# Block one of a two-block model: `w_out` and `w_ffn_out` multiplied with tokens on partitions, post-norm by token rows, result turned back

## The reference, cut to what matters

```python
h = _rmsnorm(x, g_pre_mix[l]); z = h @ w_in[l]      # then Fourier mix, window attention, memory attention
y = jnp.concatenate([norms of the three groups], axis=-1) @ w_out[l]      # [512, 1024] @ [1024, 1024]
x = x + _rmsnorm(y, g_post_mix[l])
h = _rmsnorm(x, g_pre_ffn[l])
gate, up = jnp.split(h @ w_ffn_in[l], 2, axis=-1)
f = (jax.nn.silu(gate) * up) @ w_ffn_out[l]                               # [512, 2816] @ [2816, 1024]
x = x + _rmsnorm(f, g_post_ffn[l])
```

## Time and profile before

| | us |
|---|---|
| time, median of 3 (lowest to highest) | 3827.07 (3824.5 to 3827.53) |
| profiled execution: its own time | 3827.03 |
| its span | 3825.2 |
| TensorE busy | 3566.6 (93%) |
| VectorE busy | 2516.5 (66%) |
| ScalarE busy | 1642.6 (43%) |
| mean granted TensorE clock, share of full | 0.966 |

### The profile page before, as it was taken

How to read it: one execution, slowest core, us unless ns; L and a number is a source line. 1 busy time by engine, 2 the same in 40 slices (tenths; PEclk the granted TensorE clock), 3 DMA queues, 4 the chain that set the end, 5 groups by cost and what they waited for, 6 DMA issues and landing times.

```text
span 3825.2 us, 50169 instructions
## 1 busy us (share of the span) xinstructions
PE 3566.6 (93%) x19603; PEld 2959.6 (77%) x19603; DVE 2516.5 (66%) x3593; ACT 1642.6 (43%) x2391; POOL 49.4 (1%) x67
## 2 busy tenths in 40 slices
PE   6888999888999899999899999999999989999998
PEld 4566997556898689887467789889988646788986
DVE  6548872745885498647766588639864776658853
ACT  3434552343554355424432445425542443235542
POOL 0000000000000000000000000000000000000000
PEclk8988999898999899999899999999999999999999
DMA  4112332121233223332113223232323211232331
GB/s 127 67 33 67 100 105 95 62 66 44 89 101 101 74 89 111 104 92 72 44 44 87 89 89 109 97 101 91 111 94 99 75 33 56 77 99 89 104 101 60
DMA packets 341622, 320.42 MB, mean 84 GB/s; under 512 B 10969, under 2 KB 334757, under 8 KB 341413
## 3 DMA queue, kind: packets, MB, share of 16 engines
q1 hardware_dynamic: 337204, 307.94, 25.5%
q0 software_dynamic: 2560, 8.26, 0.6%
q10 hardware_dynamic: 1648, 1.34, 0.1%
HBM read 315.40 MB, written 2.10 MB: 83 GB/s over the span
## 4 chain that ended last, share of the span: by engine, by line
PE 71%; DVE 14%; issue 11%; ACT 3%; DMA 0%; POOL 0%; ACTq 0%; DVEq 0%; POOLq 0%
PE products L712 40%; PE products L801 19%; PE small L801 3%; PE products L976 2%; DVE conv L2433 2%; DVE w_lo L1774 1%; ACT w_hi L1256 1%; DVE seven_x L1943 1%; PE small L841 1%; PE products L998 1%; PE products L860 1%; DVE X L1789 1%; DVE x_sums L1932 1%; DVE prob L2353 1%; PE products L1065 1%
## 5 line engine op out<-in xcount | busy, mean ns | idle before, releaser
L1774 DVE TENSOR_TENSOR w_lo<-raw,w_hi 128x2048 fp32r<-128x2048 f32 x192 | 439.9, 2292 | 564.1 <-ACT w_hi L1256 562.9
L1256 ACT ACTIVATE w_hi<-raw 128x2048 fp32r<-128x2048 f32 x192 | 367.3, 1914 | 974.6 <-PE products L712 974.6
L712 PE MATMUL products<-a_hi,w_hi 128*128 128x512 f32 (+1 forms) x1424 | 586.7, 412 | 58.4 <-DVE a_lo L1829 31.9
L712 PE MATMUL products<-a_lo,w_hi 128*128 128x512 f32 (+1 forms) x1424 | 574.2, 403 | 0.0
L712 PE MATMUL products<-a_hi,w_lo 128*128 128x512 f32 (+1 forms) x1424 | 573.5, 403 | 0.0
L801 PE MATMUL products<-seven_x,w_hi 128*128 128x256 f32 x2592 | 469.2, 281 | 8.4 <-DVE w_lo L1972 3.8
L712 PE MATMUL products<-h_lo,w_hi 128*128 128x512 f32 x1056 | 418.6, 396 | 0.0
L712 PE MATMUL products<-h_hi,w_lo 128*128 128x512 f32 x1056 | 418.6, 396 | 0.0
L712 PE MATMUL products<-h_hi,w_hi 128*128 128x512 f32 x1056 | 418.6, 396 | 0.0
L801 PEld LDWEIGHTS products<-seven_x,w_hi 128*128 128x128 f32 x2592 | 397.5, 189 | 12.2 <-DVE w_lo L1972 5.1
L712 PEld LDWEIGHTS products<-a_hi,w_hi 128*128 128x128 f32 (+1 forms) x1424 | 273.3, 192 | 145.0 <-issue 61.0
(11 more groups left out here) (384 smaller groups left out, 6273.9 us busy)
## 6 DMA issues: line engine op xcount, KB each, us to landing
raw<-in_ffn_w SPq DMA_DIRECT2D x240, 512.0 KB, 4.3
raw<-in_w_in SPq DMA_DIRECT2D x108, 512.0 KB, 4.9
raw<-in_w_ffn_in SPq DMA_DIRECT2D x88, 512.0 KB, 4.4
raw<-in_w_out SPq DMA_DIRECT2D x32, 512.0 KB, 4.2
raw<-in_w_ffn_out SPq DMA_DIRECT2D x32, 512.0 KB, 4.1
raw<-in_ffn_w SPq DMA_DIRECT2D x32, 384.0 KB, 3.5
raw<-in_w_ffn_out SPq DMA_DIRECT2D x16, 384.0 KB, 3.5
raw<-in_w_mem_kv SPq DMA_DIRECT2D x8, 512.0 KB, 4.1
```

What stands on the lines that cost most here:

```text
L712: mm = pe.matmul(G[pair][0:m, into + b, 0:n], w[:, s, at:at + m], x, start=(first or into > 0) and k == 0 and q == 0, stop=(last or ends) ...
L1256: act.activation(w_hi[:, s, :], raw[:, s, :], ACT.Copy).then_inc(hi_ready, 1)
L1774: dve.tensor_tensor(w_lo[:, s, :], raw[:, s, :], w_hi[:, s, :].bitcast(F32), ALU.subtract).then_inc(lo_ready, 1)
```

## The change

The two matrices are multiplied the other way round: the operand is the stationary side (128 tokens by 128 input channels), the weights are the moving side (512 output channels wide), and the result has tokens on partitions. It is made in two halves of 512 output channels, four banks each (four tiles of 128 tokens): half 0 in the four `G` banks, half 1 in `B4` to `B7`. The number of products is the same. Units are now 4 input chunks by 512 columns; `w_ffn_out` has one short unit (2 chunks, 24 products) at the end of half 0 and one at the start of half 1. The last unit of half 1 goes token tile by token tile.

ScalarE squares each bank with a running sum over its row (so no adds). The roots are then one number per partition and token tile: VectorE combines both halves, GpSimd takes the power on a 128x1 column, VectorE scales both banks of the tile from PSUM to `y_tok` in SBUF. TensorE turns 32 tiles of 128x128 back into the eight banks. Then VectorE has one operation a chunk, `xT = bank * gain + xT`, in place of two. The split of F1 is moved: on ScalarE from ahead of the post-norm to behind the eight high parts (`late_unit`), on VectorE to behind the eight low parts. The loops of these stages are written out. Removed: `copy_and_square`, `sum_channels` and `spread` of the post-norms, `y_ffn`.

```diff
+MIX_UNITS = (((2, 3, 4, 5), (0, 1, 6, 7)), ((2, 3, 4, 5), (0, 1, 6, 7)))
+FF_FOURS = tuple(tuple(range(k, k + 4)) for k in range(0, FC - 2, 4))
+FF_UNITS = (FF_FOURS + ((FC - 2, FC - 1),), ((FC - 2, FC - 1),) + FF_FOURS)
...
+        def token_banks(p):
+            return ([G[p][:, 0, :], G[p][:, 1, :], G[1 - p][:, 0, :], G[1 - p][:, 1, :]], [B4[:], B5[:], B6[:], B7[:]])
...
+            def by_tokens(hi, lo, halves, before):                      # TensorE
...
+                for half, (banks, units) in enumerate(zip(token_banks(p), halves)):
+                    for u, chunks in enumerate(units):
+                        take_unit()
+                        s, last = (c.unit - 1) % 2, u == len(units) - 1
+                        order = [(n, t) for n in range(len(chunks)) for t in range(TC)]
+                        if half and last:
+                            order.sort(key=lambda at: at[1])
...
+                            for q, (x, w) in enumerate(((hi, w_hi), (lo, w_hi), (hi, w_lo))):
+                                mm = pe.matmul(banks[t], x[:, k, t * P:(t + 1) * P], w[:, s, n * SEQ:(n + 1) * SEQ],
...
+                            if last and n == len(chunks) - 1:
+                                mm.then_inc(tok_done, 1)
...
+                pe.wait_ge(y_scaled, scaled + 2)
+                for i in range(4):
+                    for t in range(2):
+                        turn(i, t)
+                pe.wait_ge(y_scaled, scaled + 3)
+                for i in range(6):
+                    for t in (2,) if i < 4 else range(3):
+                        turn(i, t)
+                pe.wait_ge(y_scaled, scaled + 4)
+                for i in range(DC):
+                    for t in (3,) if i < 6 else range(4):
+                        mm = turn(i, t)
+                    mm.then_inc(z_ready, 1)
...
-                if post_norm:
-                    c.one("sq_used", DC)
-                    sum_channels()
-                    spread()
...
+            def operand(gain, l, squares=True, late_unit=True):         # ScalarE
...
+                if late_unit:
+                    split_hi()
                 if squares:
                     squares_of_x()
...
+            def by_tokens(halves):                                      # ScalarE
...
+                    for t in range(TC):
+                        act.wait_ge(tok_done, c.next("tok_done"))
+                        act.activation(X[:, t, :], banks[t], ACT.Square,
+                                       accum_out=stats[:, 0, half * TC + t:half * TC + t + 1]).then_inc(
...
+            def by_tokens(halves, gain, l, next_gain):                  # VectorE
...
+                for t in range(TC):
+                    dve.wait_ge(stat_ready, c.next("stat_ready"))
+                    root = mean_sq[:, t:t + 1]
+                    dve.scalar_tensor_tensor(root, stats[:, 0, TC + t:TC + t + 1], 1.0 / D, stats[:, 2, t:t + 1],
+                                             ALU.mult, ALU.add).then_inc(pow_asked, 1)
+                    dve.wait_ge(pow_done, c.next("pow_done"))
+                    dve.tensor_scalar(y_tok[:, t, 0:SEQ], first[t], root, None, ALU.mult)
+                    dve.tensor_scalar(y_tok[:, t, SEQ:D], second[t], root, None, ALU.mult).then_inc(y_scaled, 1)
+                banks = turned_banks(p)
                 for i in range(DC + 1):
                     if i < DC:
...
+                        dve.wait_ge(z_ready, c.next("z_ready"))
+                        dve.scalar_tensor_tensor(xT[:, i, :], banks[i], col(gain, l, i), xT[:, i, :],
+                                                 ALU.mult, ALU.add).then_inc(x_ready, c.one("x_ready"))
...
+                        lows_of_x(i - 1, *next_gain)
+                dve.wait_ge(tok_done, c.next("tok_done", TC))
+                split_lo()
...
+            def token_roots():                                          # GpSimd
...
+                    pool.tensor_tensor(root, root, minus_half[:, i:i + 1], ALU.pow).then_inc(pow_done, 1)
```

More of the change, by code:

```diff
@@ L1088, in _, with before @@
                 sum_groups(totals[2:])
[L1090 to L1103, removed]
+                def before(u, n, t, k):
+                    if t:
+                        return
+                    if (u, n) == (1, 2):
+                        spread_groups(totals[2:], (B6[:],))
+                    pe.wait_ge(al_ready, c.next("al_ready"))
+                by_tokens(a_hi, a_lo, MIX_UNITS, before)
                 ffn(True)
@@ L1440, in ffn @@
                             group_skipped()
[L1442 to L1449, removed]
+            def by_tokens(halves):
+                for half, (banks, units) in enumerate(zip(token_banks(c.group % 2), halves)):
+                    for _ in units[1:]:
+                        unit_done()
+                    if not half:
+                        act.wait_ge(tok_done, c.now("tok_done") + TC)
+                        split_hi()
+                    for t in range(TC):
+                        act.wait_ge(tok_done, c.next("tok_done"))
+                        act.activation(X[:, t, :], banks[t], ACT.Square,
+                                       accum_out=stats[:, 0, half * TC + t:half * TC + t + 1]).then_inc(
+                                           stat_ready, c.one("stat_ready"))
+                    act.wait_ge(stat_ready, c.now("stat_ready"))
             def latent_attention(leave):
@@ L1903, in normalised @@
                 low(n - 1)
[L1905 to L1907 removed]
+            def by_tokens(halves, gain, l, next_gain):
+                p = c.group % 2
+                first, second = token_banks(p)
+                for half, units in enumerate(halves):
+                    for u in range(len(units) - 1):
+                        piece()
+                        split_lo()
+                        if half and u == 0:
+                            dve.wait_ge(stat_ready, c.next("stat_ready", TC))
+                            stepped(dve.tensor_scalar(stats[:, 2, 0:TC], stats[:, 0, 0:TC], 1.0 / D, EPS, ALU.mult, ALU.add))
+                    if not half:
+                        dve.wait_ge(tok_done, c.next("tok_done", TC))
+                        split_lo()
+                settled()
+                for t in range(TC):
[6 more added lines that the diff above has]
+                    dve.tensor_scalar(y_tok[:, t, SEQ:D], second[t], root, None, ALU.mult).then_inc(y_scaled, 1)
+                banks = turned_banks(p)
```

116 lines of the change are left out of this document (64 added, 52 removed).

## The result

The changed kernel takes 3788.32 us (median of 4 runs, 3785.62 to 3793.4), the kernel before in the same session 3825.78 (4 runs, 3822.81 to 3827.53). The ratio is 0.9904 [0.9887, 0.9922]: 37.5 us less. The forecast was 3780.6, a gain of 46.4, and faster by over 0.2% with 0.95; the time lies in the range, 7.7 us from the forecast. The profiled execution took 3790.08 with a span of 3788.3, where before it was 3827.03 and 3825.2. TensorE is busy for 3569.0 us, as good as before (3566.6); what went is its idle time.

What follows compares the result with a forecast made beforehand. TensorE, busy 93%, was taken to idle behind each post-norm matrix's last product, 18.9 us at four places. Gains 3 x 12.2 + 9.8 = 46.4 off 3827.03 gave 3780.6 us, range 3773 to 3798.

Steps and rivals of the forecast that it cites:

- E: End of the last product of a post-norm matrix; the forecast's times are in us behind it.
- F0's clock: First 8 of F0's 48 products at the low clock as before, so F0 is through at about 19 us.
- wait at the sum: TensorE's idle time at the pre-norm's sum in F1, until VectorE's adds are done: 0.8 us.
- sum in F1: Pre-norm's sum inside F1, set by VectorE's adds: 24.3 us against 36.5, 12.2 gained at three post-norms.
- layer 0: memory tile: Behind layer 0's FFN, F1's second `memory_tile` waits for ScalarE's copy; TensorE goes on at 25.1 us, idle nearly 3.
- layer 0: gain: Behind layer 0's FFN: 11.3 us gained, less 1.5 for low clock after TensorE's idle time, 9.8.
- A: Rival: operand chunks don't overlap, 2.2 us each and not 1.33; gain 6 a place, 3805 us; chance 0.14.
- B: Rival: `w_ffn_out`'s short units or a late weight stall, up to 2 x 4 us, 3789; chance 0.05.
- C: Rival: with weights moving, each of 1440 products takes longer, e.g. 0.28 us for 0.235, 3846 us; chance 0.03.
- D: Rival: no gain, something later such as weights holds F2 or the next stage; chance 0.02.
- the clock also falls while F1 waits at the sum, 1.5 in each of three places: Smaller rival: low clock behind TensorE's wait at the pre-norm's sum, 1.5 us in three places, 3785 us.
- the likeliest case: The forecast's sum as it stands, chance 0.76; bounds on power, scaling, transposes, clock and hand-overs give 3776 to 3790.

Runs made afterwards that it cites:

- e1: The changed kernel unaltered, run and profiled once more: 3791.01 us, ratio 0.9902 to the kernel before.
- e9: The kernel before the change, unaltered, profiled once more: 3826.92 us, ratio 1.0005.
- e7: The changed kernel with eight unread products put ahead of the pre-norm's sum in F1, in the three places with a plain F1: 3778.28 us, ratio 0.987.
- e2: The changed kernel with the pre-norm's sum in F1 behind product 24 instead of 18, in the three plain places: 3774.45 us, ratio 0.9863.
- e5: The changed kernel with sum later, ScalarE's F1 split earlier, and behind layer 0's FFN later memory tiles and sum: 3769.04 us, ratio 0.9848.
- e8: Half of the change against the kernel before: `w_out` changed, the FFNs of block one as before: 3807.52 us, ratio 0.9944.
- e4: The changed kernel with the pre-norm's sum behind 24 products and ScalarE's split of F1 ahead of the high parts: 3775.57 us, ratio 0.9861.
- e10: The same kernel as e5 once more, on another chip, for a second profile: 3767.81 us, ratio 0.9849.

## Why the prediction was right or wrong

| step | forecast, us behind E | measured |
|---|---|---|
| power done | 1.75 | 1.54 |
| first `xT` starts | 3.4 | 3.41 |
| first product of F0 | 5.8 | 5.9 |
| F0's clock | low at first | 1.00 |
| F1 split done | 17.9 | 18.0 |
| wait at the sum | 0.8 | 1.88 |
| sum in F1 | 24.3 | 24.4 |
| sum to spread | as before, 5.8 | 9.0 (5.9 to 9.0 in e1) |
| layer 0: memory tile | 25.1 | 25.16 |
| layer 0: gain | 9.8 | 9.8 |

**Right.** The chain of the root, the overlap of `xT` and low part (1.32 a chunk, so A is out), the move of the split and what it delays, VectorE as the new setter of the sum, the wait of the second memory tile. The short units cost nothing (B), the products didn't get slower (C: 473 matmuls in 110 us without idle time), and the gain wasn't swallowed (D), if for a possible few us in block two (e9). At the second memory tile TensorE idled 3.61 us, not "nearly 3", and the low clock behind it cost 3.39 − 1.90 = 1.5 from there to the sum, as taken off.

**The term that was mis-sized: the clock behind the sum.** The forecast had the case, "the clock also falls while F1 waits at the sum, 1.5 in each of three places", with 3785 for it, and left it out of the sum. It measured 3.2 in each of the three places in the profile compared, 9.6 together; 4.6 in e1's. With it the sum is 36.8, against 37.0 from E to the copies of the root and 37.5 measured. Two things were wrong in it. The wait was taken as 0.8 because F0 was taken to begin at the low clock "as before"; but before, TensorE had stood for 6.4 us, and now the transposes break the time up, with nothing over 1.1. F0 ran at 1.00, so TensorE came to the sum a microsecond earlier and stood for 1.88. The forecast had that too ("if the clock stays high F0 ends at 17.3 and F1 waits 0.6", measured 0.65) and didn't carry it on to the sum. The forecast took a faster TensorE for harmless there, because VectorE sets the sum; but the engine that waits comes out of the wait slower. And the price of 1.5 was that of the eight products in the earlier trace rows (3.2 − 1.9, which is 1.3), where here some thirteen ran at 1.2 GHz, and the sum's own small products too. e7 shows the cause: with the wait filled, the loss is gone; e2 and e5 turn it into a gain.

**Small terms.** The scaling from PSUM takes 0.75 and not 0.69 (two in 1.41, forecast 1.3); the power of one column 0.54 and not 0.57. The first ten of the 14 transposes take 284.20 − 283.06 = 1.14 us from start to start of the next, 0.11 each and not 0.09. The Trainium skill ("TensorE: Matmul & The Clock Gate", "Part 4: PE-mode transpose") has about 275 ns; that is what the profile gives as the modelled duration of one row (272), while their pace is less than half of it. These small terms offset each other. The bounds of the likeliest case are added up too narrow: if the transposes' 1.1 counts in each of three places, as the wording has it, they give 3777.5 to 3792 and not 3776 to 3790. The time lies in both.

**What the forecast got for nothing.** The stages ahead of E and the start gave 4.7 + 2.25, the unchanged rest took 7.0. That they cancel is luck. So is, in part, how near 36.8 comes to 37.5: e1's profile has a loss of 4.6 in place of 9.6 and about the same time. The ranges of runs, 4.7 us before and 7.8 after, are of that size.

## What to carry to other kernels

When a chain in front of TensorE is cut short, look at the next point where it meets the other engines: it arrives there early, waits, and a wait of 1.9 us before dense products can cost 3 us more than itself in low clock. Put the meeting point behind more products (6 here took the wait from 1.88 to 0.47), or fill the wait; here the profile showed the loss only in the distance of starts and in the granted clock, not as idle time. And compare stage by stage, against a second profile of each kernel: unchanged stages here differ by up to some 6 us, more than what one of these places gains or loses by the clock.

## What the runs showed of the hardware

The same wait of 1.87 or 1.88 us at the same point of the code was followed by 0, 1.5 or 3.1 us of loss within one execution (e1), by 3.2 three times in another (after) and twice in a third (e8). Behind waits of 0.16 to 0.47 us (e2, e4, e5, e10) there was no loss, nor where products filled the wait (e7). A stage of block two whose code is the same in all kernels took from 529.4 to 535.6 us; a window of 50 us in it had a clock of 0.90 in one profile and 0.83 in another. And 32 fp32 transposes with idle times of up to 1.1 us between them left the granted clock at 1.00.
